# A decoder trunk's second input projection by one level of Strassen's scheme

## The chip, the cores and the metric

One core of one Trainium2 chip. The metric is the device time of one execution in microseconds, median of several runs. The engines are TensorE (PE in the profile, PEld for its weight loads), VectorE (DVE), ScalarE (ACT), GpSimd (POOL) and SyncE (SP), which here issues almost all DMAs.

## What is computed

One inference step of a trunk of two layers, for a prompt of 2048 tokens and 32 sample tokens (8 sequences of 4), 2080 in all; the model width is 1024 and all data are float32. Cut to what matters:

```python
for l in range(2):
    h = rmsnorm(y, norm_pre[l])
    mk, mv = mem_kv(mem_prompt, ...)           # samples: cached memory keys and values
    if l == 0:
        q, k, v, lf, xq, gate = split_fox(h @ fox_w_in)   # forgetting attention
        mix = fox(q, k, v, lf)
    else:
        u, xq, gate = split_pool(h @ pool_w_in)           # 1024 | 512 | 1536 columns
        # means over the last 2, 4, 8, 16 tokens by group of 256 channels
        mix = einsum(mean(u, w) - u, w_group) * scale
    b = concat(mix, mem_attend(xq, mk, mv)) * silu(gate)
    y = y + rmsnorm(b @ w_out[l], norm_post[l])
```

The change concerns `h @ pool_w_in`, a product of (2080 x 1024) by (1024 x 3072), and what runs beside it.

## The kernel before

Every float32 operand of a large product is split into a rounded high part and the rest (`hi`, `lo`, both float32r), and a product of 128 x 128 weights is three matmuls: hi by hi, hi by lo, lo by hi.

`decoder_step` runs these blocks one after the other: the first input projection (`project_pass` "p0") with other work beside it, the forgetting attention, the first output product (`Output` "o0"), the second input projection (`project_pass` "p1"), the second output product ("o1").

In "p1" the tokens lie in two halves of 1056 (1024 and the 32 samples) and 1024. A tile is 128 columns of `pool_w_in`; the 24 tiles are run over the first half, then again over the second (`tiles = columns * 2`), in the order memory queries (4), their gates (4), pool stream u (8), the mixer's gates (8). A tile's weights come in one DMA of 512 KB, two tiles ahead; VectorE makes `w_hi` (L336) and `w_lo` (L338); TensorE runs 8 x 3 matmuls per chunk (L393); the chunks are 384, 336 and 336 tokens wide in the first half and 512 twice in the second. Two PSUM banks take turns, ScalarE evicts them with copy or SiLU (L420) into `z_st`, and SP stores the rows into `z1` in DRAM. The normed tokens stay in SBUF: tokens 0 to 383 are normed in the last part of the first output product (`NextNorm`), the rest by `norm_rows` beside "p1" (squares L1141, scaling L1175, transposes L1189, high and low parts L1146 and L1165).

Work beside a pass is a `Work`: steps with a program for each engine, and a plan of points (place in the pass, steps done by then). `Beside.advance` issues the steps due on each engine's queue between the matmuls' own slots. All queues are in order, so a step that waits holds back what follows it on its engine. The place in "p1" counts tiles of 48; `NT` is 24. Beside it run the norms, `memory_sample` (from 24.5 to 29), `memory_attention` for the prompt (29 to 38.5, 42 steps; 32 pairs of score blocks: transposes L1300, scores L1314 to L1316, maximum L1387, exponentials L1358, products L1327 to L1329) and `pool_mixing` (38.5 to 47.95). `pool_mixing` has 16 units, each 256 channels by 512 tokens, and 23 steps: sums on VectorE (L2553) and on GpSimd (L2433), average (L2561), high part on ScalarE (L2498), low part (L2570), 12 matmuls (L2477 to L2479), scaling with the gate (L2585). The samples' part of the mixing is in it too. 17 steps are due inside the pass, the rest follow it.

## Time and profile before

| | us |
|---|---|
| median of 3 runs | 3353.71 |
| lowest, highest | 3353.24, 3357.15 |
| span of the profiled execution | 3354.0 |
| TensorE busy, VectorE busy, ScalarE busy, GpSimd busy | 3234.5, 1297.8, 1096.0, 511.4 |
| 2305.8 to 3066.1: between the output products | 760.3 |

Times in rows count from the span's start. In a row of instructions, the first number is the start or the busy time in us; a bracket or a column after "|" is the time for which the engine stood idle before, with what released it. A matmul's duration is longer than its distance to the next, since matmuls are pipelined; only distances between starts tell its cost.

### The profile page before, as it was taken

What the parts mean: (1) busy time and instruction counts of PE and PEld (TensorE: products, weight loads), DVE (VectorE), ACT (ScalarE), POOL (GpSimd) and SP (SyncE); (2) the same over time, 40 slices, a digit from 0 to 9 for tenths busy, and PEclk for the clock granted to TensorE, in tenths of its full rate; (3) what the DMA queues carried; (4) which work ended last, traced back from release to release, by engine and by line L of the source; (5) the groups of instructions that cost most, each with busy time, mean ns of one, the idle gap of its engine ahead of it and who ended that gap; (6) DMA issues with size and microseconds to landing.
All of it is one profiled execution on the core that took longest, in us unless ns stands there. A gap on an engine that the chain in (4) does not pass through costs nothing. (4 is left out here: it accounts for less than half of the span.)

```text
span 3354.0 us, 51636 instructions
## 1 busy us (share of the span) xinstructions
PE 3234.5 (96%) x19705; PEld 2772.9 (83%) x19705; DVE 1297.8 (39%) x2582; ACT 1096.0 (33%) x2157; POOL 511.4 (15%) x769
## 2 busy tenths in 40 slices
PE   7999999999999998999999999997999999996999
PEld 7999999777777777878888887886999888785887
DVE  4331223232333215545555554333222246655332
ACT  3112232122322225455666653222223244112211
POOL 3310000101111112244433330000000012211000
PEclk9999999999999999989999999999999999997999
DMA  5444533579899964443332225432333544756431
GB/s 158 126 135 144 163 110 120 162 229 304 298 325 310 305 183 141 128 126 89 92 92 85 89 73 169 132 104 82 121 108 102 172 127 145 228 162 210 132 110 56
DMA packets 409588, 515.69 MB, mean 154 GB/s; under 512 B 50855, under 2 KB 298216, under 8 KB 407919
## 3 DMA queue, kind: packets, MB, share of 16 engines
q1 hardware_dynamic: 386503, 444.68, 42.7%
q0 software_dynamic: 22848, 67.78, 6.2%
q8 instruction: 158, 2.59, 0.3%
q14 instruction: 79, 0.65, 0.1%
HBM read 388.50 MB, written 124.22 MB: 153 GB/s over the span
## 5 line engine op out<-in xcount | busy, mean ns | idle before, releaser
L420 ACT ACTIVATE z_st_p<-bank 128x512 f32<-128x512 f32 (+3 forms) x322 | 166.8, 518 | 643.5 <-PE bank L393 641.7
L393 PE MATMUL bank<-h00hi,w_hi_p 128*128 128x352 f32 x960 | 317.4, 331 | 3.9 <-DVE h00lo L1165 3.5
L1829 PE MATMUL bank<-w_hi_o,b_hi_o 128*128 128x512 f32 x782 | 305.6, 391 | 14.0 <-DVE w_lo_o L1755 14.0
L393 PE MATMUL bank<-h00hi,w_lo_p 128*128 128x352 f32 x960 | 309.3, 322 | 0.0
L393 PE MATMUL bank<-h00lo,w_hi_p 128*128 128x352 f32 x960 | 309.1, 322 | 0.0
L1830 PE MATMUL bank<-w_hi_o,b_lo_o 128*128 128x512 f32 x782 | 305.4, 390 | 0.0
L1831 PE MATMUL bank<-w_lo_o,b_hi_o 128*128 128x512 f32 x782 | 305.3, 390 | 0.0
L835 PE MATMUL bank<-pT_fa,v_fa 128*128 128x256 f32 x1092 | 272.0, 369 | 4.4 <-issue 2.4
L393 PE MATMUL bank<-h01hi,w_hi_p 128*128 128x512 f32 x640 | 266.7, 417 | 0.0
L336 DVE CAST w_hi_p<-w_raw_p 128x1024 fp32r<-128x1024 f32 x128 | 89.0, 696 | 422.1 <-PE bank L393 392.9
L393 PE MATMUL bank<-h01hi,w_lo_p 128*128 128x512 f32 x640 | 251.3, 393 | 0.0
L393 PE MATMUL bank<-h01lo,w_hi_p 128*128 128x512 f32 x640 | 250.2, 391 | 0.0
L2275 DVE COPY kT_sf<-bank 128x512 f32<-128x512 f32 x128 | 88.5, 692 | 349.3 <-PE bank L2203 349.3
L874 ACT COPY pT_fa<-bank 128x512 f32<-128x512 f32 (+2 forms) x320 | 163.0, 520 | 183.5 <-PE bank L850 182.0
L835 PEld LDWEIGHTS bank<-pT_fa,v_fa 128*128 128x128 f32 x1092 | 190.8, 190 | 26.5 <-issue 3.9
L393 PEld LDWEIGHTS bank<-h00hi,w_hi_p 128*128 128x128 f32 x960 | 181.1, 189 | 9.8 <-issue 5.4
L1829 PEld LDWEIGHTS bank<-w_hi_o,b_hi_o 128*128 128x128 f32 x782 | 147.6, 189 | 46.2 <-DVE w_lo_o L1755 14.4
L393 PEld LDWEIGHTS bank<-h00lo,w_hi_p 128*128 128x128 f32 x960 | 181.5, 189 | 0.6
L393 PEld LDWEIGHTS bank<-h00hi,w_lo_p 128*128 128x128 f32 x960 | 181.1, 189 | 0.0
L2244 ACT COPY kT_sf<-bank 128x512 f32<-128x512 f32 x128 | 75.0, 586 | 319.5 <-PE bank L2203 319.5
L850 PE MATMUL bank<-ident_const,sc_fa 128*128 128x128 f32 x1088 | 174.0, 276 | 4.3 <-ACT pT_fa L874 2.8
L1830 PEld LDWEIGHTS bank<-w_hi_o,b_lo_o 128*128 128x128 f32 x782 | 147.5, 189 | 30.8
(341 smaller groups left out, 6862.6 us busy)
## 6 DMA issues: line engine op xcount, KB each, us to landing
k_raw_sf<-in_cache_fox_k SPq DMA_DIRECT2D x128, 512.0 KB, 5.3
v_raw_sf<-in_cache_fox_v POOLq DMA_DIRECT2D x128, 512.0 KB, 6.0
z<-z_st_p SPq DMA_DIRECT2D x112, 512.0 KB
w_raw_p<-in_fox_w_in SPq DMA_DIRECT2D x80, 512.0 KB, 5.2
b_raw_o<-bT SPq DMA_DIRECT2D x32, 768.0 KB, 6.2
w_raw_p<-in_pool_w_in SPq DMA_DIRECT2D x48, 512.0 KB, 5.1
out<-tok_p SPq DMA_DIRECT2D x64, 256.0 KB, 4.2
w_raw_o<-z SPq DMA_DIRECT2D x62, 256.0 KB, 2.8
```

The source lines that it names most:

```text
L336: nc.vector.tensor_copy(w_hi[:, u, :, 0:width], w_raw[:, u, :, 0:width]).then_inc(whi_d, 1)
L393: last = nc.tensor.matmul(bank[:, 0:width], wt[:, u, k, :], h[:, k, at0:at0 + width], start=(m == 0), stop=(m == MM - 1))
L420: nc.scalar.activation(z_st[0:rows_t, t % 2, at0:at0 + width], bank[0:rows_t, 0:width], tiles[t][2]).then_inc(z_read, 1)
L835: last = nc.tensor.matmul(OUT[J % 2][0][:, c0:QW], vn, pT[:, J % 2, n, c0:QW], start=(n == 0), stop=(n == QB * (j + 1) - 1))
L850: last = nc.tensor.transpose(T_BANKS[g % 2][:, n * P:(n + 1) * P], sc[:, qt % NB, (4 * p + n) * P:(4 * p + n + 1) * P], ident[:, :])
L874: nc.scalar.copy(pT[:, J % 2, 4 * p:4 * p + nk, a * P:(a + 1) * P], T_BANKS[g % 2][:, 0:nk * P].rearrange("p (n q) -> p n q", q=P)).then_i ...
L1829: nc.tensor.matmul(bank(t, half)[:, :], bh, w_hi, start=(k == 0), stop=False)
L1830: nc.tensor.matmul(bank(t, half)[:, :], bl, w_hi, start=False, stop=False)
L1831: last = nc.tensor.matmul(bank(t, half)[:, :], bh, w_lo, start=False, stop=(k == NK - 1))
L2244: nc.scalar.copy(kT[:, s // 2 % 2, 0:4, s % 2 * P:(s % 2 + 1) * P], T_BANKS[0][:, :].rearrange("p (h n) -> p h n", h=4)).then_inc(ka_d, 1)
L2275: nc.vector.tensor_copy(kT[:, s // 2 % 2, 4:8, s % 2 * P:(s % 2 + 1) * P], T_BANKS[1][:, :].rearrange("p (h n) -> p h n", h=4)).then_inc(k ...
```

## The change

The product is cut into 2 x 2 blocks: input channels in two halves (`kh`), columns in pairs of tiles, tokens of a group in two chunks (`ch`). A pair of tiles by two chunks then takes seven block products of half depth (4 x 3 matmuls) for eight, on sums and differences of the weights and of the tokens.

- The tokens are in three groups: 640 and the samples (chunks of 336), then twice 704 (chunks of 352). Each group runs over 12 pairs of tiles; a place in the plans now counts pairs of 36.
- Weights: one DMA of 1 MB per pair. GpSimd makes four sums per pair (`weight_sum`), ScalarE rounds each of the seven blocks of 128 x 512 (`high`), VectorE subtracts (`low`), three products ahead, with four buffers.
- Tokens: per group seven blocks `t_hi` and `t_lo` are built, by ScalarE and VectorE (`build`), from the raw normed tokens and sums (VectorE's in group 0, GpSimd's after). In group 0 this happens in the first pair, for a later group in the last pair of the group before.
- Results: three PSUM banks. ScalarE evicts two products of a pair, VectorE adds the other five to partial results (`combine`), and ScalarE applies SiLU to stored rows where there is a gate (`gate`).
- Norms: `NextNorm` now does tokens 0 to 639 and the samples in the first output product (six tiles for three) and leaves them unsplit; the samples are tile 5 of that product instead of its last. `norm_later` norms tokens 640 up beside the pass and stores them transposed in DRAM (`hT`); a group is loaded from there by one DMA when the tenth pair of the group before begins.
- Beside the pass: the samples' mixing is a work of its own (`pool_sample`, 10 steps), the prompt's memory attention is cut in two works of 26 steps and 16 pairs of score blocks, and `pool_mixing` takes units of the first two token chunks first and waits for rows unit by unit. `memory_sample` keeps a PSUM bank less, which adds one wait for the batch before. Works use PSUM banks 3 to 7.
- `nc.all_engine_barrier()` is added before and after the pass.

The diff, cut to its core:

```diff
+FIRST = 5 * P
+def strassen_pass(nc, tag, banks, w, groups, columns, zT, bufs, raw, tmp, later, rows, works):
+    NP, NG, KH, R, Q = len(columns) // 2, len(groups), KT // 2, 4, 2
+    N = NG * NP * 7
+    A11, S2, S3, A12, S1, A22, S4 = range(7)
+    BUILT = [[0, 1, 2, 3, 4, 5, 6] if g == 0 else [0, 2, 3, 1, 4, 5, 6] for g in range(NG)]
+    BUILD_AT = [1, 3, 4, 5, 5, 6, 7]
...
+        def accumulator(m):
+            q, i = divmod(m, 7)
+            role = "ABCADCD"[i]
+            return banks[{"A": 0, "B": 1 + q % 2, "C": 2 - q % 2, "D": 1 + q % 2}[role]]
...
+            def weight_sum(q, n):
+                if q:
+                    pool.wait_ge(wlo_d, 7 * (q - 1) + (S1, S2, S3, S4)[n] + 1)
...
+                nc.gpsimd.tensor_tensor(w_sum[:, n, :, :], a, b, op).then_inc(sum_d, 1)
...
+            def low(m):
+                dve.wait_ge(whi_d, m + 1)
+                nc.vector.tensor_tensor(w_lo[:, m % R, :, :], stationary(m), w_hi[:, m % R, :, :].bitcast(F32), ALU.subtract).then_inc(wlo_d, 1)
+            def build(g, x):
+                i, wd = BUILT[g][x], groups[g].width
+                dve.wait_ge(thi_d, 7 * g + x + 1)
+                nc.vector.tensor_tensor(t_lo[:, i, :, 0:wd], moving(g, i), t_hi[:, i, :, 0:wd].bitcast(F32), ALU.subtract).then_inc(tlo_d, 1)
+            def first_sums():
+                nc.vector.tensor_tensor(t, h(0, 1, 1), h(0, 0, 1), ALU.subtract).then_inc(tsum_v, 1)
+                low(0)
+                build(0, 0)
+                nc.vector.tensor_tensor(h(0, 0, 1), h(0, 0, 1), h(0, 0, 0), ALU.subtract).then_inc(tsum_v, 1)
...
+                nc.vector.tensor_tensor(h(0, 0, 0), t, h(0, 0, 0), ALU.add).then_inc(tsum_v, 1)
+            def combine(m):
...
+                dve.wait_ge(z_done, m + 1)
+                nc.vector.tensor_tensor(out, a, bank[:, 0:wd], ALU.add).then_inc(dve_d, 1)
...
+            for n, q, i, half, at in slots():
+                if half == 0:
+                    if n:
+                        combine(n - 1)
+                    if n + R - 1 < N:
+                        low(n + R - 1)
+                    for g, x in builds(n):
+                        build(g, x)
+                beside.advance(at)
...
+                    pe.wait_ge(wlo_d, n + 1)
+                    if p == 0:
+                        pe.wait_ge(tlo_d, 7 * g + BUILT[g].index(i) + 1)
...
+                    elif i in (S2, S3) and q:
+                        pe.wait_ge(dve_d, 5 * (q - 1) + (4 if i == S2 else 5))
+                    elif i in (S1, A22, S4):
+                        pe.wait_ge(dve_d, 5 * q + {S1: 1, A22: 2, S4: 3}[i])
+                for m in range(3 * KH * half // Q, 3 * KH * (half + 1) // Q):
+                    k, term = divmod(m, 3)
+                    st = (w_lo if term == 2 else w_hi)[:, n % R, k, :]
+                    mv = (t_lo if term == 1 else t_hi)[:, i, k, 0:wd]
...
 def memory_sample
-                if b >= 2:
-                    pe.wait_ge(o_d, b - 1)
+                if b:
+                    pe.wait_ge(m_d, b)
...
 class NextNorm:
-    AT = (5, 8, 11)
+    AT = (5, 6, 8, 9, 11, 12)
...
 def pool_mixing
-    units = [(g, 2 * half + k) for half in range(2) for g in range(G) for k in range(2)]
+    units = [(g, ch) for ch in range(2) for g in range(G)] + [(g, ch) for g in range(G) for ch in range(2, NC)]
...
-            project_pass(nc, "p1", const, banks, pool_w_in, halves, tiles, z1, bufs, rows, [norm, sample, prompt, mixing])
+    norm_later     [(0.6, 0), (7.8, 14)]
+    memory_sample  [(8, 0), (13, 14)]
+    pool_sample    [(13.3, 0), (15.8, 10)]
+    front, prompt_memory chunks 0 and 1   [(15.8, 0), (17.2, 8), (20.9, 26)]
+    back, prompt_memory chunks 2 and 3    [(28.4, 0), (31.6, 26)]
+    pool_mixing    [(31.6, 0), (33.4, 12), (34.4, 14), (35.4, 16), (35.99, 17)]
+            strassen_pass(nc, "p1", banks, pool_w_in, GROUPS, tiles, z1, bufs, raw1, tmp1, later, rows, [norm, sample, new, front, back, mixing])
+        nc.all_engine_barrier()
```

The six lines with works and their plans stand for calls of the same content.

## Rows read from the trace of the kernel before

**Rows 1.** The page, busy time: engine, busy us and share, instructions.

```profile
PE 3234.5 (96%) x19705; PEld 2772.9 (83%) x19705; DVE 1297.8 (39%) x2582; ACT 1096.0 (33%) x2157; POOL 511.4 (15%) x769
```

**Rows 2.** Windows: stretch, length, busy us by engine, clock, DMA share, GB/s.

```profile
2305.80:2318.60 12.80, 0.42 (x2) 0.00 (x0) 5.00 (x9) 0.88 (x3) 0.00 (x0) 0.70 0.43 123
2318.60:2618.50 299.90, 295.15 (x1841) 293.48 (x1842) 84.19 (x118) 77.75 (x153) 0.00 (x0) 0.99 0.34 110
2618.50:2705.20 86.70, 86.70 (x578) 68.87 (x577) 25.87 (x55) 23.88 (x51) 0.95 (x1) 1.00 0.60 191
2705.20:2856.10 150.90, 149.26 (x801) 125.44 (x800) 87.60 (x146) 77.00 (x201) 36.37 (x32) 1.00 0.42 133
2856.10:3018.80 162.70, 153.66 (x688) 126.07 (x686) 98.33 (x138) 27.62 (x37) 40.46 (x52) 0.97 0.66 198
3018.80:3066.10 47.30, 19.57 (x48) 14.10 (x48) 28.63 (x30) 6.59 (x8) 11.05 (x8) 0.67 0.59 182
```

**Rows 3.** TensorE's waits from 2305.8 to 3066.2: us in total, times, longest.

```profile
PE bank L2477 <- DVE mix_pm L2585: 22.7, 8, 6.1
PE bank L1829 <- DVE w_lo_o L1755: 14.0, 1, 14.0
PE bank L393 <- DVE w_lo_p L338: 12.4, 1, 12.4
```

**Rows 4.** Timeline, ScalarE: evictions that end two tiles of either half.

```profile
2390.59 0.46 ACT L420 ACTIVATE z_st_p<-bank 128x336 f32<-128x336 f32 x1 [3.25 <-PE bank L393]
...
2402.22 0.45 ACT L420 ACTIVATE z_st_p<-bank 128x336 f32<-128x336 f32 x1 [3.25 <-PE bank L393]
...
2866.96 0.60 ACT L420 ACTIVATE z_st_p<-bank 128x512 f32<-128x512 f32 x1 [4.84 <-PE bank L393]
...
2877.84 0.60 ACT L420 ACTIVATE z_st_p<-bank 128x512 f32<-128x512 f32 x1 [4.84 <-PE bank L393]
```

**Rows 5.** Timeline of the opening: weights asked for, rounded, and the first matmul.

```profile
2312.72 1.01 SPq L254 DMA_DIRECT2D w_raw_p<-in_pool_w_in  x2
...
2316.61 0.69 DVE L336 CAST w_hi_p<-w_raw_p 128x1024 fp32r<-128x1024 f32 x1 [6.22 <-DMA w_raw_p<-in_pool_w_in]
...
2318.61 0.69 PE L393 MATMUL bank<-h1ahi,w_hi_p 128*128 128x384 f32 x1 [12.39 <-DVE w_lo_p L338]
```

**Rows 6.** Windows after the first matmul, columns as in rows 2.

```profile
2322.00:2324.00 2.00, 2.00 (x8) 2.00 (x7) 0.81 (x1) 1.15 (x2) 0.00 (x0) 0.50 0.75 204
2324.00:2326.00 2.00, 2.00 (x13) 1.97 (x12) 0.15 (x1) 0.00 (x0) 0.00 (x0) 0.88 0.81 254
```

**Rows 7.** Instructions by line, whole span: ns min/median/max, first and last start.

```profile
L338 DVE TENSOR_TENSOR w_lo_p<-w_raw_p,w_hi_p x128: 1224/1226/2193, 14.6 to 2992.2; 128x1024 fp32r<-128x1024 f32 x128
...
L1377 DVE TENSOR_TENSOR pT_lo_ma<-bank,pT_hi_ma x64: 671/692/695, 1276.8 to 2849.8; 128x512 fp32r<-128x512 f32 x64
...
L2553 DVE TENSOR_TENSOR acc_pm<-u_pm x16: 694/700/1593, 2879.8 to 3038.2; 128x526 f32<-128x526 f32 x16
...
L1387 DVE TENSOR_REDUCE nm_ma<-bank x64: 669/682/692, 1270.1 to 2843.3; 128x2 f32<-128x512 f32 x64
...
L1274 POOL TENSOR_TENSOR pr_ma<-pr_ma,rr_ma x64: 1038/1041/3014, 1272.1 to 2845.3; 128x512 f32<-128x512 f32 x64
```

**Rows 8.** VectorE's waits, 2650 to 3020: us in total, times, longest.

```profile
DVE rr_ma L1400 <- ACT pr_ma L1358: 26.5, 32, 1.1
```

**Rows 9.** Timeline of VectorE in the tail: an average, and the low part after it.

```profile
3023.62 1.23 DVE L2561 SCALAR_TENSOR_TENSOR dd_pm<-acc_pm,u_pm 128x1024 f32<-128x1024 f32 x1
3026.64 1.63 DVE L2570 TENSOR_TENSOR d_lo_pm<-dd_pm,d_hi_pm 128x1024 fp32r<-128x1024 f32 x1 [1.79 <-ACT d_hi_pm L2498]
```

**Rows 10.** Timeline of TensorE in the tail: first matmuls of the last three units.

```profile
3029.09 0.77 PE L2477 MATMUL bank<-d_hi_pm,wg_hi_pm 128*128 128x512 f32 x1 [3.61 <-DVE mix_pm L2585]
...
3037.75 0.65 PE L2477 MATMUL bank<-d_hi_pm,wg_hi_pm 128*128 128x512 f32 x1 [3.20 <-DVE mix_pm L2585]
...
3047.11 0.76 PE L2477 MATMUL bank<-d_hi_pm,wg_hi_pm 128*128 128x512 f32 x1 [4.78 <-DVE mix_pm L2585]
```

## What the change should do to the time

> **What bounds the kernel now.** The page comes first: TensorE is busy nearly the whole span [rows 1]. Busy time hides gaps here, because one matmul's duration overlaps the next, so I went on to the stretches around the second input projection (windows of the trace) and to what ended each wait of TensorE in them. From the last matmul of the first output product (2305.8) to the first of the second (3066.1) there are 760.3 us in six stages [rows 2]: 12.8 us of opening gap, 299.9 for the first half of the tokens, 86.7 with the samples' memory attention beside, 150.9 with the prompt's, 162.7 with the mixing, and a tail of 47.3 in which only the mixing's last four units run. TensorE's waits with a name sum to 12.4 us at the opening and 14.0 before the second output product, and 22.7 are waits for the mixing, that is for VectorE [rows 3]. Inside the pass the projection sets the pace. A tile of the first half takes 11.62 us and one of the second 10.88 where nothing runs beside it, from eviction to eviction [rows 4]. Only the product's columns can give a large gain, and each engine's work per matmul stage decides how much of it arrives.
>
> **The projection itself.** Before: 24 x 11.62 + 24 x 10.88 = 540.0 us. A first-half tile streams 24 x (384 + 336 + 336) columns, 10.56 us at 2.4 GHz, so a matmul costs 14.7 ns beside its columns (72 of them); in the second half it is 13.3 ns. After: 12 pairs of tiles x 7 products x 12 matmuls, 336 columns wide in group 0 and 352 in groups 1 and 2. At 14.5 ns beside the columns a product lasts 1.86 or 1.93 us, a pair 13.0 or 13.54, the pass 12 x 13.0 + 24 x 13.54 = 481 us. **The saving is 59 us**; the eighth of the columns alone would be 62.
>
> **Old losses that go.** The first half took 299.9 us for 278.9 of tiles. Thirteen norm tiles beside it cost TensorE some 0.9 us each, 11.4; the other 9.6 are cold clock and first waits, and the old form of both is gone. The mixing stage took 162.7 for ten tiles (108.8), 12 units of 12 matmuls of 512 columns (32.7) and about 4 us of the samples' part: 17.2 are waits and clock. These 26.8 us leave with the old schedule; what takes their place is counted in full below. Everything else that TensorE does there (21.4 us of the sample attention, 63.9 of the prompt's 32 steps, the mixing's matmuls) stays as it is. The tail of 47.3 stays too: the last four units are the same four, and they run at VectorE's pace.
>
> **Opening, +6.** Now: weights are asked for at 2312.7, VectorE starts on them at 2316.6, TensorE at 2318.6 [rows 5]. After, the first load is twice as large (+2, between 0 and 4), then come ScalarE's half of a weight block and of a token block and VectorE's rest of both, 0.6 + 1.4 + 1.65 in a row where 2.0 stood (+1.8), one more barrier (+1, between 0 and 3), and a last store of 128 rows for one of 32 (+1). Range 3 to 10.
>
> **First pair, +10.** Its seven token blocks are built while it runs. VectorE needs 1.23 us for 1024 elements [rows 7], hence about 1.65 for 1344, and has two sums, then 0.6 + 1.65 per product: the second product waits some 3.5 us for it, the first two run at the lower clock, which lasted about 6 us after the opening gap [rows 6], and the rest go at VectorE's 2.7 to 2.9 us a product. I get 22.8 us from first to last matmul against 13.0. Range 6 to 16.
>
> **Steady pairs, 0.** Per pair VectorE splits seven weight blocks (0.61 each, start to start) and adds five results (0.45): 6.5 us of 13.5. ScalarE rounds seven blocks and evicts two, about 5. The tightest loop is S4, which waits until VectorE has read S1, one product (1.93 us) earlier, for a step of 0.5. Weights are split three products ahead. So a step of other work on VectorE that lasts longer than some 4 to 6 us stops TensorE. That is new: before, weights were two tiles ahead and VectorE read no result.
>
> **Group changes, +3.** Seven builds of 1.65 on top of 0.93 a product make VectorE and ScalarE 17 us busy in a pair of 13; both run up to 5 us behind and use up the lead of three products. Range 0 to 10. **Norms, +2:** eleven tiles in 7.2 pairs, 2.3 us of VectorE each, within the lead. Two of the thirteen old tiles move into the output product, +1.8 there and -1.8 here. Its queue on SP is moved past nothing that is urgent: weights are loaded two pairs ahead.
>
> **Samples, +4.** Their part of the mixing is 20 short sums and eight averages in one step of VectorE, about 7.5 us, and a split of the group weights of 3.5; each overruns the lead a little. The memory attention of the samples has five products a step. Range 2 to 10.
>
> **Prompt's memory attention, +11.** A step costs TensorE 2.0 us. The first half gets 1.44 products a step, 4.8 us in all, against a VectorE loop of 0.69 + 0.68 + 0.35 + 0.34, 1.1 of waiting for the exponentials [rows 8] and 1.34 for the projection: 4.7, so +3 for jitter. The second half gets 26 steps in 3.2 pairs, 0.86 product each: TensorE 3.66, VectorE about 4.1, over 18 steps +8. Range 3 to 25.
>
> **Mixing, +37, the largest term.** The plan gives it 4.4 pairs where it had 9.5 tiles: 59.6 us of projection instead of 103. One unit's loop on VectorE is serial: sums, average, 1.8 us of waiting for ScalarE's rounding, the low part, two results [rows 9]. In the tail, with nothing else on VectorE, a unit with four levels took 8.66 and 9.36 us from matmul to matmul [rows 10]; a level less is 0.72 less, so 6.6, 7.3, 8.1 and 9.0, mean 7.7. Eight units come one per 1.05 product: VectorE 7.7 + 1.0 = 8.7, TensorE 2.0 + 2.7 = 4.7, a loss of 32, less the lead of three products, 26. The next five have 3.6 products each: VectorE 53.8, TensorE 48.5, a loss of 5. With TensorE half idle the clock will fall at times, as it did in the tail (granted 0.67 [rows 2]); 6 us for that, between 0 and 15. **Second barrier, +1.**
>
> **A rule that speaks against the change.** In this trace a VectorE subtraction that reads only SBUF varies from 1.22 to 2.19 us and the mixing's sums from 0.69 to 1.59, while one with an operand in PSUM stays within 0.67 to 0.70; GpSimd's own product varies from 1.04 to 3.01 [rows 7]. The Trainium skill, SBUF — State Buffer, section Who interferes with whom, says that VectorE with two inputs in SBUF and a GpSimd instruction that reads SBUF exclude each other for a whole instruction; the trace agrees, with the rows just named. The change puts 144 weight sums on GpSimd, at 1.04 us 150 us in all, beside 252 weight splits of that kind. Their order (a sum starts when a split ends) lets most fall between splits, so I charge nothing; fully excluded they would add 0.6 us per product to VectorE, which costs nothing in a steady pair (10.7 of 13.5) but about 9 us in the dense attention and 18 in the mixing. That is the first rival.
>
> **Sum.** -59 - 26.8 + 6 + 9.8 + 3 + 2 + 4 + 11 + 37 + 1 = -12. The profiled execution spans 3354.0 us and the median is 3353.7, so both give **3342 us**.
>
> **Rivals.** (1) **VectorE's port**, slower: the price just named, 27 us, and it decides once GpSimd's sums meet more than about half of the splits in these two stages; the sum then is +15, with the upper bounds of the mixing's clock and the opening +25: 3360 to 3380, point **3370**. For it: the spread of the rows. Against: in steady pairs there is room. (2) **Losses even out**: first pair, attention and mixing each a few us dearer, +12 together: **3354**. For it: every price is at least as likely low as high, and three of them rest on a loop that no row shows at this density. (3) **The waits are covered**, much faster: between units VectorE catches up more than I allow, the old 26.8 go, and of the new losses only opening, first pair and 20 us of mixing stay: -59 - 27 + 17 + 26 = -43, **3311**. Against it: the tail's periods are pure VectorE time. (4) **Narrow products bring no time**, a floor per matmul above 161 ns: 3024 matmuls stand where 2880 stood. The clean tiles exclude it at 336 columns. 0.02, within the slower side.
>
> **Chances.** Forecast (3328 to 3347) 0.35, rival 3 (below 3328) 0.13, rival 2 (3347 to 3360) 0.20, rivals 1 and 4 (above 3360) 0.32. A measurement of this kernel tells 0.2%, about 7 us, from no change: faster 0.48, same 0.20, slower 0.32. The forecast's own range is 3328 to 3347; the range for 8 in 10 takes in most of the rivals, 3314 to 3380.
>
> **What would show it.** After's profile: clean pairs of 13.0 and 13.5 us between evictions of A11 and a pass of about 613 us of TensorE work; an opening near 18.5; a first pair near 23. TensorE's waits on VectorE in the pass should lie in the mixing, in eight steps 8 to 9 us apart, with the clock below 1.00 there. Weight splits near 0.7 mean speak for the forecast, near 1.2 for rival 1. If pairs without other work take 14.5 or more, the tight loop of S4 is wrong; if the attention's second half shows no waits, its term is; if the mixing's dense units come every 5 to 6 us, rival 3 is right.

## The result and the profile after

The changed kernel takes 3434.18 us (median of 4, 3431.03 to 3434.82) against 3355.43 for the kernel before, run on the same chip (median of 4, 3353.24 to 3357.56). The ratio is 1.0235, with a 95% interval of 1.0221 to 1.0250: **slower by 79 us**, where 3342 and a range of 3314 to 3380 were forecast. The profiled execution spans 3432.6 us. The page shows that TensorE became less busy and everyone else busier [rows 1]:

```profile
PE 3208.1 (93%) x19865; PEld 2781.0 (81%) x19865; DVE 1576.7 (46%) x2934; ACT 1247.2 (36%) x2411; POOL 764.1 (22%) x922
```

So the projection did become cheaper, by the matmuls. Two clean pairs of the third group show it, from one eviction of A11 to the next (timeline of ScalarE):

```profile
2835.18 0.45 ACT L758 COPY part_p<-bank 128x352 f32<-128x352 f32 x1 [0.78 <-PE bank L719]
2848.52 0.45 ACT L758 COPY part_p<-bank 128x352 f32<-128x352 f32 x1 [0.78 <-PE bank L719]
```

That is 13.34 us for 7 x 12 matmuls of 352 columns; 13.54 were forecast. What was lost stands beside it. TensorE's waits from 2300 to 3200 (us in total, times, longest), to be held against [rows 3]:

```profile
PE bank L3054 <- DVE mix_pm L3124: 35.2, 10, 7.5
PE bank L719 <- DVE t_lo_p L650: 22.8, 2, 18.1
PE bank L719 <- DVE z_st_p L679: 22.8, 10, 10.1
PE bank L2306 <- DVE w_lo_o L2232: 16.5, 1, 16.5
PE bank L719 <- DVE part_p L679: 14.7, 4, 5.6
PE bank L1966 <- DVE out_all_sm L2017: 11.8, 5, 4.8
PE bank L3054 <- DVE d_lo_pm L3115: 7.9, 1, 7.9
PE bank L719 <- issue: 6.0, 3, 2.9
PE bank L1763 <- DVE pT_lo_mb L1842: 5.8, 9, 1.8
PE bank L1752 <- DMA kv_raw_mb<-out: 4.1, 1, 4.1
```

Eight of the ten lines end with VectorE. L679 is `combine`, the additions that empty the banks of the pass; no matmul waits for a weight split of the pass (L645). Before, all named waits of this stretch made 55 us, 49 of them in the three lines of [rows 3]; here they make 161, of which these ten lines are 148. The opening (t_lo_p, 18.1) is one of them. Windows of five stretches, columns as in [rows 2]: the opening, the first four products of the first pair, the second change of group, the pairs with the mixing, and the tail:

```profile
2306.50:2325.00 18.50, 0.40 (x3) 0.03 (x1) 8.57 (x10) 3.34 (x6) 4.42 (x3) 0.57 0.42 142
2325.00:2344.50 19.50, 11.13 (x48) 10.20 (x48) 17.66 (x14) 8.91 (x12) 12.33 (x6) 0.71 0.17 54
2780.00:2805.00 25.00, 16.35 (x88) 16.38 (x89) 24.75 (x22) 10.43 (x16) 12.55 (x7) 0.80 0.21 72
2970.00:3091.00 121.00, 92.90 (x440) 82.64 (x441) 96.89 (x120) 31.84 (x49) 50.02 (x38) 0.88 0.60 182
3091.00:3145.00 54.00, 20.89 (x56) 14.55 (x54) 31.38 (x32) 7.51 (x8) 15.21 (x11) 0.69 0.50 157
```

In the third, VectorE is busy for 24.75 us of 25.00 and TensorE for 16.35: that is a change of group, which I had put at 1.5 us. VectorE's subtractions and GpSimd's sums of weights have these durations (ns min/median/max of each line, then first and last start); the counterpart of before is in [rows 7]:

```profile
L645 DVE TENSOR_TENSOR w_lo_p<-w_sum_p,w_hi_p x144: 675/693/3294, 2329.9 to 3085.6; 128x512 fp32r<-128x512 f32 x144
L645 DVE TENSOR_TENSOR w_lo_p<-w_raw_p,w_hi_p x108: 677/968/3515, 2321.1 to 3078.0; 128x512 fp32r<-128x512 f32 x108
...
L601 POOL TENSOR_TENSOR w_sum_p<-w_raw_p x72: 1264/1298/2583, 2320.5 to 3056.8; 128x512 f32<-128x512 f32 x72
L601 POOL TENSOR_TENSOR w_sum_p<-w_sum_p,w_raw_p x36: 1260/1559/2483, 2321.8 to 3053.8; 128x512 f32<-128x512 f32 x36
L601 POOL TENSOR_TENSOR w_sum_p<-w_raw_p,w_sum_p x36: 1277/1661/2593, 2326.1 to 3064.0; 128x512 f32<-128x512 f32 x36
```

Undisturbed a split takes 0.69 us; half of the second kind take 0.97 or more, and single ones five times as long. Two rows of pair 24, where nothing runs beside the pass, show what happens (timeline of GpSimd and VectorE):

```profile
2810.32 1.30 POOL L601 TENSOR_TENSOR w_sum_p<-w_raw_p 128x512 f32<-128x512 f32 x1 [5.87 <-DVE w_lo_p L645]
...
2811.10 1.07 DVE L645 TENSOR_TENSOR w_lo_p<-w_raw_p,w_hi_p 128x512 fp32r<-128x512 f32 x1
```

The sum ends at 2811.62 and the split at 2812.17, 0.55 us later. The rest are the same: 55 of the 252 splits overlap with exactly one weight sum; 31 of them began while the sum ran, and every one ended 0.55 us after it; in the other 24 the sum began last and ended 1.13 to 1.16 us after the split. So one instruction runs its length and holds the other up, whichever began first.

**The ledger.** To see which term failed, I cut the 838.5 us between the output products at the evictions of A11 and put the forecast's own terms for each stretch beside them. (Forecast of pairs 8 to 15, for instance: 4 x 13.0 + 4 x 13.54 + 25.4 of the samples' TensorE work + 4 + 1.5 = 137.1.) The last column is experiment e2 below, in which GpSimd reads no SBUF for the pass.

| stretch | forecast | after | e2 |
|---|---|---|---|
| opening | 18.8 | 18.5 | 17.5 |
| first matmul to A11 of pair 1 | 24.7 | 31.5 | 26.1 |
| pairs 1 to 7 (norms) | 102.9 | 108.4 | 106.5 |
| pairs 8 to 15 (samples, first change of group) | 137.1 | 166.3 | 157.5 |
| pairs 16 to 22 (attention, front) | 129.8 | 138.2 | 133.7 |
| pairs 23 to 27 (second change, then clean) | 69.2 | 79.2 | 69.0 |
| pairs 28 to 31 (attention, back) | 94.2 | 107.7 | 105.1 |
| pair 32 to the end of the pass (mixing) | 121.8 | 133.7 | 119.8 |
| tail, to the next output product | 48.3 | 55.1 | 54.9 |
| sum | 746.8 | 838.6 | 790.1 |

The forecast was 92 us too low. 48 of them go when GpSimd stops reading for the pass, and the other 43 don't. (In e2 GpSimd still reads for the memory attention and for the mixing.)

### The profile page after: what moved, and what is told of

Same layout as the page of the kernel before. It is cut to its first block and busy times, and to the rows that moved or that the text cites. A ratio compares the mean times of both kernels' runs of the same rounds, so it can differ in the third digit from the quotient of the medians.

```text
span 3432.6 us, 53641 instructions
## 1 busy us (share of the span) xinstructions
PE 3208.1 (93%) x19865; PEld 2781.0 (81%) x19865; DVE 1576.7 (46%) x2934; ACT 1247.2 (36%) x2411; POOL 764.1 (22%) x922
## 5 line engine op out<-in xcount | busy, mean ns | idle before, releaser
L719 PE MATMUL bank<-t_hi_p,w_hi_p 128*128 128x352 f32 (+1 forms) x1008 | 338.0, 335 | 66.5 <-DVE t_lo_p L650 22.8
L719 PE MATMUL bank<-t_lo_p,w_hi_p 128*128 128x352 f32 (+1 forms) x1008 | 332.2, 330 | 0.0
L719 PE MATMUL bank<-t_hi_p,w_lo_p 128*128 128x352 f32 (+1 forms) x1008 | 331.9, 329 | 0.0
L719 PEld LDWEIGHTS bank<-t_hi_p,w_hi_p 128*128 128x128 f32 x1008 | 198.7, 197 | 78.2 <-issue 76.7
L422 ACT ACTIVATE z_st_p<-bank 128x352 f32<-128x352 f32 (+2 forms) x202 | 104.5, 518 | 369.2 <-PE bank L395 367.3
L601 POOL TENSOR_TENSOR w_sum_p<-w_raw_p 128x512 f32<-128x512 f32 x72 | 110.4, 1534 | 571.3 <-DMA w_raw_p<-in_pool_w_in 309.5
L1192 PEld LDWEIGHTS bank<-pT_fa,v_fa 128*128 128x128 f32 x1092 | 191.2, 191 | 26.3 <-issue 4.0
L719 PEld LDWEIGHTS bank<-t_lo_p,w_hi_p 128*128 128x128 f32 x1008 | 198.0, 196 | 1.2
L719 PEld LDWEIGHTS bank<-t_hi_p,w_lo_p 128*128 128x128 f32 x1008 | 197.8, 196 | 0.0
```

Of the source, the lines that this page charges most:

```text
L422: nc.scalar.activation(z_st[0:rows_t, t % 2, at0:at0 + width], bank[0:rows_t, 0:width], tiles[t][2]).then_inc(z_read, 1)
L601: nc.gpsimd.tensor_tensor(w_sum[:, n, :, :], a, b, op).then_inc(sum_d, 1)
L719: last = nc.tensor.matmul(bank[:, 0:wd], st, mv, start=(m == 0 and i in (A11, S2, S3, S1)), stop=(m == 3 * KH - 1), skip_group_check=True)
L1192: last = nc.tensor.matmul(OUT[J % 2][0][:, c0:QW], vn, pT[:, J % 2, n, c0:QW], start=(n == 0), stop=(n == QB * (j + 1) - 1))
```

## Experiments

Times are medians of 4 runs unless said otherwise, beside runs of the kernel before on the same chip (3355 or 3356 in every group). The interval of a ratio is about 0.17% either way, so two variants are told apart by their times from about 6 us; below that I go by the pairs in the traces.

**e1_write_only_sums: GpSimd writes and doesn't read.** This kernel leaves the 144 weight sums out.

```diff
-                nc.gpsimd.tensor_tensor(w_sum[:, n, :, :], a, b, op).then_inc(sum_d, 1)
+                nc.gpsimd.memset(w_sum[:, n, :, :], 0.01).then_inc(sum_d, 1)
```

> The changed kernel, but GpSimd's 144 weight sums are left out: in each one's place stands a fill of the same 128x512 block, which only writes. Waits, places in the queues and all of VectorE's instructions stay. Theory A (GpSimd's sums hold VectorE's subtractions up at a port that both read through; in the changed kernel the 252 weight splits take 0.90 to 1.07 us against 0.68 for an undisturbed one, 73 us in all, and more falls on the token builds): the splits come back to 0.68 to 0.72 mean, the losses in samples, group changes, attention and mixing shrink, and the time falls by 40 to 70 us, to 3365 to 3395 us. Theory B (the order of VectorE's queue alone: steps of other work longer than the lead of three products stop TensorE whatever else runs): the splits get shorter but the long steps stay, and the time falls by less than 25 us, to 3410 or more. The Trainium skill, SBUF - State Buffer, section Who interferes with whom, says that an instruction of GpSimd that only writes does not disturb a VectorE instruction with two inputs in SBUF; if it holds, theory A's first number is seen here.

Measured: 3397.98 us, ratio 1.0133 (1.0116 to 1.0150), 36 us less than the changed kernel; 3 us above the range of theory A and 12 below that of B. The splits' mean fell from 0.90 and 1.07 us to 0.79 and 0.83, not to the 0.68 to 0.72 expected: GpSimd's products in the memory attention, its sums in the mixing and its token sums still read. The 23 splits that overlap with a fill alone take 0.69 us on the mean, like those that overlap with nothing. The gain lies in the mixing (11.8 us in pairs 32 to 34), the samples (9.3), the attention (7.3), the first pair (3.5) and a change of group (3.3), and **nothing** of it in pairs without other work: pairs 24 to 27 take 53.0 us here and 52.9 there. A fill is also shorter (0.53 us for 1.57 on the mean), so an earlier weight sum may be in the 36 too. Only a small part is seen: ScalarE's waits for a weight sum are 7.6 us in six places in the changed kernel, 3.1 of them in the opening and just behind it, and 1.0 us here.

**e2_no_pool_reads: the sums of the tokens also as fills.** All sums of GpSimd for the pass are left out.

```diff
-                    nc.gpsimd.tensor_tensor(t, h(g, 1, 1), h(g, 0, 1), ALU.subtract).then_inc(tsum_p, 1)
+                    nc.gpsimd.memset(t, 0.01).then_inc(tsum_p, 1)
```

(and so for the other three)

> As e1_write_only_sums, and the token sums of GpSimd at the group changes are left out too, again with a fill of the same block in their place. The second group change (tenth to twelfth pair of the second group) takes a pair of 26.3 us in the changed kernel where 13.35 is clean. Theory A: that pair falls to 14 to 17 us, and the time is 5 to 15 us below e1_write_only_sums. Theory B (VectorE and ScalarE have 17 us of work in a pair of 13 there): the pair stays above 20 us, and the time is within 5 us of e1_write_only_sums.

Measured: 3387.05 us, ratio 1.0099 (1.0082 to 1.0116). Pair 23, the change of group, fell from 26.3 us (23.0 in e1) to 17.2. The same two lines as above, here:

```profile
L645 DVE TENSOR_TENSOR w_lo_p<-w_sum_p,w_hi_p x144: 676/692/1328, 2327.1 to 3037.8; 128x512 fp32r<-128x512 f32 x144
L645 DVE TENSOR_TENSOR w_lo_p<-w_raw_p,w_hi_p x108: 674/692/1317, 2321.3 to 3030.4; 128x512 fp32r<-128x512 f32 x108
```

The longest split is 1.3 us where it was 3.5; in e1 it was still 3.5, beside a token sum. The forecast's first rival was right in its mechanism, and too cheap in all: 47 us, not 27. Where it gave a price it was too dear: 27 us for the mixing and the back half of the attention, where the ledger's last two columns differ by 13.9 and 2.6. Two thirds of the 48 lie in stretches for which it gave none. Pair 23 needs a caution. A token sum takes 3.2 to 3.7 us and its fill 1.3, and ScalarE waits 4.7 us for one in the changed kernel, 2.5 in e1 and not at all here; how much of that pair's 9 us is VectorE held up, and how much is GpSimd's own time, no run separates.

**e10_before_sums_beside: the same load beside the old schedule.** 144 sums on GpSimd with buffers of their own, added to the kernel before:

```diff
+        for n in range(count):
+            pool.wait_ge(done, n + 1)
+            nc.gpsimd.tensor_tensor(out[:, :], a[:, 0, :], a[:, 1, :], ALU.add).then_inc(done, 1)
+            yield
```

> The kernel before, with 144 additions of 128x512 on GpSimd (two inputs of SBUF, own buffers, results unused) spread evenly over the second projection; nothing else changes. Theory of the tight loop: the same port contention lengthens VectorE's splits here too (from 1.45 us by a quarter or more at the mean), but TensorE has a lead of one tile and a bank in hand and doesn't see it: 0 to 10 us, 3355 to 3365. Rival, contention costs the same under any schedule: 30 us or more, 3385 or more.

Measured: 3373.95 us, ratio 1.0055 (1.0039 to 1.0072), so 18.7 us: between the two. Lines by group from 2300 to 3100, first the kernel before, then e10 (busy us, mean ns | idle before):

```profile
L338 DVE TENSOR_TENSOR w_lo_p<-w_raw_p,w_hi_p 128x1024 fp32r<-128x1024 f32 x48 | 65.5, 1366 | 1.6
```

```profile
L354 DVE TENSOR_TENSOR w_lo_p<-w_raw_p,w_hi_p 128x1024 fp32r<-128x1024 f32 x48 | 78.1, 1628 | 1.6
...
L166 POOL TENSOR_TENSOR out_sb<-a_sb 128x512 f32<-128x512 f32 x144 | 222.2, 1543 | 8.5
```

GpSimd's sums are held up as much as in the changed kernel (1.54 us mean), the splits by 0.26 us each. Following the evictions of the tiles, counted from the first one of the pass, shows where it costs: e10 is 5.5 us behind after the first 40 us (norms), still 5.5 behind some 330 us later, with the rest of the norms and the samples' memory attention in between, 7.7 behind as the mixing begins, and 18.8 behind at the end of the pass. In those 330 us VectorE is busy 8.7 us longer than before (93.7 for 85.0) and it costs nothing; in the mixing it is busy 14 us longer (105.2 for 91.1) and that costs 11, with no wait of VectorE or ScalarE for GpSimd, so GpSimd being late itself isn't the cause. Under the new schedule it is as uneven: from e2 to the changed kernel VectorE's busy time grows by 7.1 us in pairs 24 to 27 for 1.1 us of time, and by 8.7 us in pairs 32 to 34 for 13.7. What the new schedule adds is that the first pair, the samples, the attention and the changes of group pay as well: outside the mixing the ledger's last two columns differ by 35 us of 48, and here it is 8 of 19.

**e6_lead_five: a longer lead for the weights.**

```diff
-    NP, NG, KH, R, Q = len(columns) // 2, len(groups), KT // 2, 4, 2
+    NP, NG, KH, R, Q = len(columns) // 2, len(groups), KT // 2, 6, 2
```

> Six weight buffers instead of four: the high and low parts of the weights are made five products ahead of TensorE instead of three; nothing else changes. Theory: TensorE waits for VectorE's additions of the product one back (they set both the banks and the order), not for weights, so a longer lead for weights brings 0 to 10 us, 3424 to 3434, and the waits for the results stay. Rival, late weight splits are the stall: 20 us or more come back, 3414 or less, and waits on part and staging tiles shrink with it.

Measured: 3420.72 us, ratio 1.0190 (1.0173 to 1.0207), 13.5 us less: between the two. It came in pairs 13 to 15 (5.2 us), 28 to 31 (4.1) and 32 to 34 (6.8); pairs 16 to 20 lost 3.8. The waits for the banks hardly moved (z_st_p 22.8 to 19.7, part_p 14.7 to 12.9); the two for the mixing fell more (mix_pm 35.2 to 31.4, d_lo_pm 7.9 to 3.4). No wait named a weight split, and yet making the splits earlier brought time. I read it so: a part of what the profile books as a wait for VectorE's last step is a split that stands ahead of that step in its queue, and the releaser named is the last one and not the cause. The traces don't show that by themselves.

**e17_lead_no_reads: lead and no contention** (the edits of e2 and of e6 together).

> Six weight buffers together with GpSimd's weight and token sums as fills that only write (3387.1 us with four buffers); the output is therefore not the reference's. The longer lead alone brought 13.5 us where GpSimd reads. Theory of overlap: it hides splits that contention makes late, and without contention it brings 5 us or less: 3382 to 3388. Rival: it hides VectorE's other work too, and brings its 10 to 14 us here as well: 3373 to 3377.

Measured: 3379.52 us, ratio 1.0069 (1.0052 to 1.0086), 7.5 us less than e2. Again between the two: of the 13.5 us that the lead brings with contention, 7.5 are left without it. About half would then be contention hidden, and the other half VectorE's other work.

**e3_mixing_behind: how much the cover is worth.**

```diff
-                                 [(31.6, 0), (33.4, 12), (34.4, 14), (35.4, 16), (35.99, 17)],
+                                 [(36, 0), (36.1, 1)],
```

> The changed kernel with one plan altered: all steps of the prompt's mixing stand behind the pass, nothing is left out. In the changed kernel the last four pairs take some 135 us with twelve units of the mixing beside them, where four clean pairs and the twelve units' matmuls need 86. If VectorE's serial loop of a unit is what sets the pace beside the pass as well as alone (mine), the four pairs come down to 54 us, and the sixteen units then take 7 to 8.5 us each behind it, some 95 us more of tail than now, plus about 15 us for loads and the group weights: the time rises by 20 to 40 us only, to 3455 to 3475 us, though no matmul of the projection covers the mixing any more. If the mixing was covered as such work is in the kernel before, the time rises by its whole length, 80 us or more.

Measured: 3462.61 us, ratio 1.0322 (1.0305 to 1.0340), 28.4 us more than the changed kernel, as expected. Pairs 32 to 34 go from 119.7 us to 40.6, and yet only 28 us are lost. The twelve units that run beside the pass save no more than 28 us over running alone, when VectorE paces them anyway. Alone the sixteen units come 8.5 us apart on the mean (from 3025.14 to 3152.14).

**e4_mixing_in_two: eight units moved to pairs 24 to 28**, where the changed kernel has clean pairs; the rest stay, and the group weights are split a second time (2.3 us of VectorE for their low part).

```diff
-    STEPS = LEAD + NU + 3
+    PH, HU = LEAD + NU // 2 + 3, NU // 2
+    STEPS = 2 * PH
...
-                                 [(31.6, 0), (33.4, 12), (34.4, 14), (35.4, 16), (35.99, 17)],
+                                 [(24.15, 0), (28.3, 15), (31.6, 15), (32.6, 19), (33.4, 20), (34.4, 21), (35.4, 23), (35.99, 24)],
```

> The changed kernel with the mixing in two parts: the eight units of the first two token chunks run in pairs 24.15 to 28.3, which have no work beside them now, ahead of the second part of the memory attention, and the other eight stay in pairs 31.6 to 36 and behind. Nothing is left out; the group weights are split a second time. The dense stage (eight units, one for each product) is gone: a unit has 3.5 products. By the prediction's arithmetic of VectorE (7.7 us a unit and 1 us a product, against 2.7 and 1.93 for TensorE) some 26 us of the mixing's loss go and 5 to 10 come back as single stops: 3410 to 3422 us. If each unit costs TensorE a stop of its own, however far apart they are, as VectorE's queue is blocked for 7 us against a lead of less than 6, no more than 10 us are won: 3424 us or more.

Measured: 3441.60 us, ratio 1.0260 (1.0243 to 1.0277), 7 us more than the changed kernel, so the first expectation failed and its rival, a stop for each unit, held. Pairs 24 to 27 went from 52.9 us to 120.2, pairs 32 to 34 from 119.7 to 58.1. My text had the pace wrong: 15 steps over 4.15 pairs are one per 1.94 products. But at nearly twice the room that they had before, the units cost no less. TensorE's waits from 2300 to 3200:

```profile
PE bank L3057 <- DVE mix_pm L3128: 39.7, 8, 8.9
PE bank L719 <- DVE z_st_p L679: 29.2, 13, 10.0
```

The waits for the mixing became fewer and longer, and the additions of the pass (L679) are late more often, 13 times for 10. The loss goes **with the work put in**, and spreading it out doesn't lower it.

**e12_samples_spread: the same question for the samples.** Their memory attention over 7.6 pairs instead of 5, their pooling alone in pairs 25 to 28.

```diff
-                sample, ends_s = sample_memory(1, s1, room, z1, D, D + XW + D, [(8, 0), (13, 14)], rows.when(XP - 1))
+                sample, ends_s = sample_memory(1, s1, room, z1, D, D + XW + D, [(8, 0), (15.6, 14)], rows.when(XP - 1))
...
-                                          [(13.3, 0), (15.8, 10)], rows.when(NP - 1), after(ends_s, 1))
+                                          [(25, 0), (28, 10)], rows.when(NP - 1), after(ends_f, 2))
```

> The memory attention of the samples takes its 14 steps over pairs 8 to 15.6 instead of 8 to 13, and the pooling of the samples goes from pairs 13.3 to 15.8 to pairs 25 to 28, where nothing else runs; nothing is left out. In pairs 8 to 15 the changed kernel loses 16.4 and 19.1 us over clean products and the works' own TensorE time, 11.8 of it in the wait of the samples' products for the output of the batch before. The same wait with the same banks costs 0.4 us in the first projection, where a step comes every 28 us. Theory: the pace makes that wait; at a step every 8 us it falls to 5 us or less and pairs 8 to 15, with pairs 25 to 28, give 8 to 15 us back: 3419 to 3426. Rival: each step stops TensorE at any pace (as the eight units of the mixing did when they were moved ahead), 3431 to 3440.

Measured: 3436.65 us, ratio 1.0246 (1.0228 to 1.0265), no gain, as the rival had it. Pairs 8 to 15 with 24 to 27 take 222.7 us for 219.2, and the wait is there with fewer, longer pieces (2440 to 2720):

```profile
PE bank L1966 <- DVE out_all_sm L2017: 12.9, 4, 7.2
```

The theory of pace fell again.

**e14_products_first: what makes that wait.** In a step TensorE transposes one batch's output, VectorE multiplies it by the gate, and TensorE's next products go to the same bank and wait for that: a round trip inside one step. Here the products come first.

```diff
-            b = batch(i, 4)
-            if b is not None:
-                pe.wait_ge(o_d, b + 1)
...
-                nc.tensor.transpose(X_BANK[b % 2][:, 0:P], o_sb[:, b % 2, :], ident[:, :]).then_inc(x_d, 1)
...
-                    pe.wait_ge(m_d, b)
+                    pe.wait_ge(o_d, b)
+                if b >= 2:
+                    pe.wait_ge(m_d, b - 1)
...
+                nc.tensor.transpose(X_BANK[b % 2][:, 0:P], o_sb[:, b % 2, :], ident[:, :]).then_inc(x_d, 1)
```

> In a step of the samples' memory attention TensorE makes the products with V ahead of the last transposition instead of behind it, so that the product waits for an output of the step before and no longer for one that VectorE makes inside this step; nothing else changes. The slower pace left this wait as it was (12.9 us in 4 waits). Theory: it is a round trip from TensorE to VectorE and back inside one step, which costs whatever stands in VectorE's queue; it falls from 11.8 us to 3 or less, pairs 8 to 15 from 166.3 to 154 to 160, the time to 3421 to 3429. Rival: VectorE is late anyway in these pairs, and the time goes into TensorE's waits for the additions on the banks of the pass, 3431 to 3437.

Measured: 3426.90 us, ratio 1.0214 (1.0197 to 1.0231), 7.3 us less, as the theory had it. The longest of TensorE's waits from 2440 to 2620 are these, and none is for `out_all_sm` any more (two for DMAs make 2.0 us):

```profile
PE bank L719 <- DVE z_st_p L679: 9.9, 2, 6.9
PE bank L719 <- DVE part_p L679: 4.0, 1, 4.0
```

Pairs 8 to 15 fell from 166.3 us to 157.7. Of the 11.8 us of the wait some 3 came back as waits for the additions (13.9 here, 10.4 before in the same stretch).

**e9_finer_sample: smaller pieces.** The samples' pooling in five steps for one.

```diff
-    STEPS = 10
+    ORDER = [0, 1, 2, 3, 3.25, 3.5, 3.75, 3.9, 4, 5, 6, 7, 8, 9]
+    STEPS = len(ORDER)
...
-                                          [(13.3, 0), (15.8, 10)], rows.when(NP - 1), after(ends_s, 1))
+                                          [(13.3, 0), (15.8, 14)], rows.when(NP - 1), after(ends_s, 1))
```

> The pooling of the sample tokens in five steps instead of one: its 20 short sums on VectorE, one block of about 7.5 us in pair 14 (31.7 us, clean 13.5), are spread over the same pairs in four steps of 2 to 8 sums and one of the 8 differences. Theory: a VectorE block holds TensorE up by its own length less about 1.5 us, one product of cover, so smaller blocks let cover come in several times: pairs 13 to 15 lose 5 to 10 us of their 19, 3424 to 3429. Rival, what counts is the total of VectorE work put in, whatever its pieces: pairs 13 to 15 stay at 63 us within 2, and the time at 3431 to 3437.

Measured: 3434.34 us, ratio 1.0231 (1.0214 to 1.0248), nothing, as the rival had it. In place of one pair of 31.7 us there are two of 26.0 and 23.5, and pairs 13 to 15 take 64.2 us for 63.2. The total of VectorE's work counts here, its pieces don't.

**e16_back_spread: the same for the attention**, with the mixing behind the pass as in e3.

```diff
-                back, ends_b = prompt_memory(1, "mb1", s1, room, z1, D, D + XW + D, [(28.4, 0), (31.6, 26)], ready, after(ends_f, 2), range(2, 4))
+                back, ends_b = prompt_memory(1, "mb1", s1, room, z1, D, D + XW + D, [(28.4, 0), (35.6, 26)], ready, after(ends_f, 2), range(2, 4))
```

> The mixing wholly behind the pass, as in the kernel of 3462.6 us, and in the room this leaves the second half of the prompt's memory attention takes its 26 steps over pairs 28.4 to 35.6 (1.94 products a step) instead of 28.4 to 31.6 (0.86); nothing is left out. There its own TensorE work waits 15.5 us: 5.8 for the low parts of the probabilities, 4.1 for the keys and values, 3.1 for the queries, 2.5 for the results. Theory of density, the forecast's: with twice the products between two steps VectorE is back in time, the waits fall to 5 us or less, pairs 28 to 34 from 148.5 to 135 to 140, and the time is 3450 to 3455. Rival, each step stops TensorE at any pace, as with the samples: 145 or more for these pairs, 3459 to 3466.

Measured: 3457.07 us, ratio 1.0303 (1.0286 to 1.0320), 5.5 us less than e3. Pairs 28 to 34 went from 148.5 us to 139.9, in a profiled execution that was the fastest of four (3452.89), so the 8.6 us are rather a high reading. The theory of density is missed by 2 us and its rival by 2. TensorE's waits, first e3 (2860 to 2975), then e16 (2860 to 3000):

```profile
PE bank L1763 <- DVE pT_lo_mb L1842: 5.8, 9, 1.8
PE bank L1752 <- DMA kv_raw_mb<-out: 4.1, 1, 4.1
PE bank L1777 <- DVE q_lo_mb L1846: 3.2, 5, 1.2
PE bank L1790 <- DVE mix_mb L1860: 2.3, 7, 0.6
```

```profile
PE bank L719 <- DVE z_st_p L679: 7.6, 3, 3.7
PE bank L1777 <- DVE q_lo_mb L1846: 1.9, 1, 1.9
```

Density did make the attention's own waits (15.4 to 1.9), but 7.6 us of waiting for the additions took their place. Here the pace counts for 5 to 9 us and the rest stays.

**e8_sums_kept: a repair.** GpSimd makes the weight sums for the first group only; SyncE keeps them in DRAM and reads them back.

```diff
+            def keep(q, n):
+                sp.wait_ge(sum_d, 4 * q + n + 1)
+                sp.dma_start(kept[q, n].rearrange("p (k c) -> p k c", c=P), w_sum[:, n, :, :]).then_inc(kept_d[n], 16)
+
+            def back(q, n):
+                sp.wait_ge(wlo_d, 7 * (q - 1) + (S1, S2, S3, S4)[n] + 1)
+                sp.wait_ge(kept_d[n], 16 * q)
+                sp.dma_start(w_sum[:, n, :, :], kept[q % NP, n].rearrange("p (k c) -> p k c", c=P)).then_inc(kept_d[n], 16)
```

> The weight sums are made by GpSimd for the first group of tokens alone; SyncE stores each of those 48 tiles (256 KB) in DRAM and reads it back for the second and third group, so 96 of the 144 reading sums on GpSimd become transfers. Theory of the port: VectorE's splits are held up only while GpSimd reads SBUF. Taking all 144 sums away brought 36 us, of which the pairs of the first group held about 5; so 25 to 33 us come back and the time is 3401 to 3410, with splits of the second and third group at a mean under 0.8 us. Rival, the transfers take GpSimd's place: 128 transfers of 256 KB more, waits for them on ScalarE and a longer SyncE queue give the gain back, 3420 or more, and TensorE then shows waits behind a DMA.

Measured: 3410.76 us, ratio 1.0164 (1.0147 to 1.0181), 23.4 us less, just short of the 25 to 33 that the theory of the port gives. The splits of the second and third group have a mean of 0.83 us, where under 0.8 was expected. A part is given back, as the rival had it, in a wait behind a DMA in pairs 8 to 12 (110.3 us for 103.1); in the changed kernel the waits for these keys make 0.2 us:

```profile
PE bank L1975 <- DMA k_raw_sm<-in_cache_mem_k: 7.3, 3, 4.2
```

**e13_three_together** (kept sums, six buffers, the spread samples of e12) and **e15_kept_lead_first** (kept sums, six buffers, the order of e14).

> The kept weight sums, six weight buffers and the spread samples in one kernel. If the three act on different stalls their effects add: 24 us, 13 us and what the spread samples give; with 8 to 15 for these 3382 to 3389. If the longer lead and the missing contention cover the same late splits, less than the sum: 3392 or more. Either way it stays above the kernel before (3355), because the work of the mixing and of the attention still stands beside seven products with one product of cover.

> Kept weight sums, six weight buffers, and the samples' products ahead of the transposition, with the samples back in their pairs of the changed kernel. The three with the slower samples came to 3403, 7 us less than the kept sums alone. If the effects add, 3410.8 less 13.5 less what the order brings (5 to 13): 3384 to 3392. If the order brings nothing and lead and kept sums overlap as they seem to have done: 3398 to 3406.

Measured: 3403.04 us (ratio 1.0140, 1.0122 to 1.0158) and 3400.13 us (1.0139, 1.0122 to 1.0156). The gains alone are 23.4, 13.5 and 7.3 us, 44 together; e15 has 34. They overlap, as e17 suggests: a part of the lead's gain is contention hidden. For both kernels the expectation that the gains add (3382 to 3389, 3384 to 3392) failed, and the other (3392 or more, 3398 to 3406) held. No version came near the kernel before; e15 is the best of those that compute the whole, and 45 us slower.

## Why the prediction failed, step by step

**Right.** The saving of the projection: clean pairs are 13.3 us in groups 1 and 2. The opening: 18.5 us, 18.8 forecast. Whether the old losses of 26.8 us went, no run shows apart from what replaced them. Right in its sum was the largest term, the mixing: its dense units start on TensorE at these times (timeline; the next ones are at 2998.07, 3005.87, 3013.18 and 3025.59), which answer to [rows 10]:

```profile
2970.39 0.76 PE L3054 MATMUL bank<-d_hi_pm,wg_hi_pm 128*128 128x512 f32 x1 [7.90 <-DVE d_lo_pm L3115]
...
2978.83 0.47 PE L3054 MATMUL bank<-d_hi_pm,wg_hi_pm 128*128 128x512 f32 x1 [0.53 <-DVE mix_pm L3124]
...
2987.53 0.47 PE L3054 MATMUL bank<-d_hi_pm,wg_hi_pm 128*128 128x512 f32 x1 [3.77 <-DVE mix_pm L3124]
```

The plan has seven dense units, where the forecast counted eight. Their six distances are 9.2 us on the mean, and 8.7 in e2, for 8.7 forecast; with no contention from the pass the stretch takes 119.8 us for 121.8. Some of this is luck. The forecast put a unit alone at 7.7 us and the pass's own work at 1.0; e3, where the units run alone, has 8.5 a unit, which leaves the pass next to nothing.

**"I charge nothing" for VectorE's port: the largest error, 48 us.** This is the step that failed. The trace of before had shown the disturbance, and I argued it away with the order of the work: a sum starts when a split ends. The order doesn't keep them apart. Even in pairs 24 to 27, where VectorE has nothing but the pass, 13 of 28 splits overlap with a sum and their mean is 0.98 us; it costs nothing there because VectorE has time to spare (busy 38.2 us of 52.9). Where VectorE also serves the samples, the attention, the mixing or a change of group, TensorE waits for it and pays. The rival was in the text with its mechanism, 27 us and a chance of 0.32 together with one other; it had the mixing and the back attention, and it left out the changes of group (10 us at the second, with the caution of e2), the samples (9), the first pair (5.4 of the 6.8 us by which it is over) and the front attention (4.5). That contention alone can cost this is shown by e10; its share of the 48 is less sure, since a fill is also shorter than a sum. What the Trainium skill says (SBUF — State Buffer, Who interferes with whom: VectorE with two SBUF inputs contends with GpSimd instructions that read SBUF, and not with those that only write it) agrees with e1 and e2 in both halves: splits beside a fill alone take 0.69 us, and with fills in place of all the pass's sums the longest split fell from 3.5 to 1.3 us.

**Samples, +4: measured +33, an error of 29 us.** 8.8 of it is contention. 8.6 is the round trip of e14, which stands in the diff as two changed lines (`X_BANK` inside `O_BANK`, and the wait `m_d` for `o_d`) and which I priced at nothing without naming a cover. The first projection of the changed kernel has the same wait, for 0.4 us; VectorE is busy there for 24% of the time between the first and the last such step, against 72% here. No run has the line beside the old second projection. The two gains may overlap, since this wait is 7.6 us in e2 where it was 11.8. So 12 us or more are left; nothing but steps of VectorE is named for them, and e9 and e12 show that neither pieces nor pace take them away.

**"Steady pairs, 0": true for pairs, false as a rule for others.** The text held that a step of VectorE's longer than 4 to 6 us stops TensorE, and shorter ones don't. In e4, e9 and e12 no such threshold shows: smaller pieces and wider spacing brought nothing. My reading is that what another work puts on VectorE stands ahead of an addition for which TensorE waits one product later. I take that to be behind the norms (+5.5 us over forecast, 1.9 of it contention), a part of the samples and a part of the attention.

**Attention, +11: measured about +33.** The front half is 8 us over, half of it contention. The back half is 13.5 over: 2.6 contention; by e16 the TensorE work of its 16 steps is near 36 us and not 32 (139.9 less seven pairs of 13.5 and 9.5 of waits), which makes 4. About 7 are left. In e2 14 of the 27 splits there are still held up, by 7.3 us in all, beside GpSimd's own products of the attention, which no run takes away; so density and this contention are both possible. The forecast's VectorE loop there has slips of its own: it takes 1.1 us for each wait for the exponentials, the longest of [rows 8], where 26.5 us in 32 make 0.83, and for the front half its terms add up to 4.5 and not 4.7.

**Changes of group, +3:** pair 23 loses 12.8 us by itself, and 3.7 in e2, of which pair 24 gives back 2 (11.5 us for 13.5). Pairs 23 to 27 together take 69.0 us in e2 for 69.2 forecast, so the term was rightly sized but for GpSimd's sums. (Its own numbers, 7 x 1.65 and 7 x 0.93, make 18 us and not 17.) **The tail, "stays too": 7 us over**, and contention has no part in it. 4 of them are that the pass ends 6.2 us ahead of the tail's first unit, where the gap was 2.2 before; 3 lie between the last unit and the output product, for which the forecast had 1.

**What stays open.** About 12 us in the samples and some 7 in the back attention are put down to VectorE's queue because nothing else is named in the waits, not because a run took them away. What GpSimd's reads cost apart from the length of its sums stands open too; a run with fills stretched to a sum's length would tell. That the additions themselves are the cause, that is that more banks would remove these losses, wasn't tried: the works use the other five.

## What to carry to other kernels

A change that saves on the busiest engine by moving work to the others must be priced at the moments when those are already loaded; in the stages where they are idle it always looks free. Here 59 us of saved columns bought 144 more sums on GpSimd and 180 additions on VectorE for which TensorE waits one or two products later, and with that other work on VectorE could stop TensorE. If the trace of before shows an instruction that varies by a factor of two, give the long value as a bound in every stage where both engines are busy, and look in a diff for waits inside one step that go to another engine and back.

## What the runs showed of the hardware

- GpSimd's sum of two 128x512 inputs took 1.26 us at the least and 1.57 on the mean (144 of them) beside VectorE's splits; a split of 128x512 took 0.68 us at the least and up to 3.5. With fills for all of the pass's sums (0.53 us for a weight sum), the splits' longest was 1.3 us.
- A split that began while one weight sum ran ended 0.55 us after it, 31 times of 31; a sum that began during a split ended 1.13 to 1.16 us after it, 24 times of 24. A split beside a fill alone took 0.69 us on the mean (23 in e1), as without any.
- In e10, where 48 splits of 128x1024 took 0.26 us more each, the pass fell behind by nothing in 333 us with VectorE busy for 28% of the time, and by 11 us in the mixing, with VectorE busy for 69%.
- Matmuls of 352 columns with new weights each time come 158.8 ns apart (13.34 us for 84), 12.1 ns more than their columns at 2.4 GHz, against 13.3 at 512 columns: no floor under narrow matmuls at this width.
- With TensorE waiting for a third to nearly half of the time, its granted clock was 0.71 in the first four products and 0.80 in the change of group, a mix of its two levels of 1.2 and 2.4 GHz; both losses contain that.
